# Gate and up blocks: one 512-column product per high weight tile, the halves of a result added on VectorE

## The chip, the cores and the metric

The kernel runs on one core of a Trainium2 chip, in one launch. The metric is the time of one execution in device microseconds (us), the median of three runs. Engines are named as in the profile: PE is TensorE (PEld its weight loads), DVE is VectorE, ACT is ScalarE, POOL is GpSimd, SP issues most of the DMAs. The memories are SBUF and, for products, PSUM (`ps`), in banks of 512 columns.

## The reference, cut to what matters

Two transformer blocks run one after the other on 256 tokens and 16 meta tokens, width 1024. The change touches the gated feed-forward at the end of the second block. There only the 256 real tokens count:

```python
f = rmsnorm_2(h, norm_ffn_g[i])
h = h + (jax.nn.silu(f @ w_gate[i]) * (f @ w_up[i])) @ w_down[i]
out = rmsnorm_2(h, norm_final_g)
```

`w_gate` and `w_up` are 1024 x 2816, `w_down` is 2816 x 1024, all float32. Everything ahead of it (a hybrid mixer, a retrieval of experts by gathers from memory, sparse attention, a convolution) is the same in both kernels.

## The kernel before, in words

Float32 products are made of three faster ones. Each operand is split into a high part, which is the value rounded to the type float32r, and a low part, the rest. The result is high x high + high weight x low operand + low weight x high operand.

Weights arrive from memory in blocks of 128 x 1024, which hold 128 output columns and all eight chunks `c` of the inner dimension. A ring has four slots for raw blocks (`ring`), and as many for the high parts (`w_hi`) and the low parts (`w_lo`). SP's queue loads a block when the low part of the block four before it has been made. ACT copies the high part (`split_hi`, L395). DVE subtracts to get the low part (`split_lo`, L403). Both helpers are called through `ahead(b)`, which treats block b + 2, two blocks ahead of the one in hand. A high copy may go once PE has begun the third block before it, since only then its slot is free.

The stage in question has 44 blocks, numbered from 0: in turns of four, two of gate and two of up. There are eleven turns. The first (turn 0) and, on DVE, the last (turn 10) are written out; the others are passes of a loop on the engine's sequencer. For each block PE runs 24 products of 256 columns (`column_block`, L624): for each c the high weights with the operand's high part (`peer_x[0]`, in `x_peer`) and with its low part (`peer_x[1]`, in `x_lo`), then for each c the low weights with the high part. They add up in one of four PSUM banks. Block 0 (`chunked_block`) has its products in another order, since it starts while its operand is still being made. Between turns 0 and 1 stand 16 small products of `open_sums` (L1080).

What happens to a finished tile k of a turn (k = 0 and 1 gate, 2 and 3 up) is ordered by the code of each engine, and each engine works in the order of its code. On DVE (`hidden_tiles`): `ahead` for the tile, which is the low part of block k + 2; then the product of tile and `rstd` out of PSUM (L2629), which frees the bank (`tile_taken`); then, for k = 2 and 3, gate times up (L2634), which gives a tile of `hidden`. On ACT (`gate_tiles`): `ahead` for the tile, then, for k = 0 and 1, Silu on what DVE has left (L1774). So ACT makes the high copy for tile k + 1 only behind the Silu of tile k, and DVE makes the low part, and takes the next tile, only behind that copy.

The 22 blocks of `w_down` follow (`row_tile`, L1093): per block 12 products of 512 columns, whose stationary operand is a piece of `hidden`, split by ACT (L1784) and DVE (L2610). The first two such subtractions stand in DVE's last turn of the stage, behind gate times up of tiles 2 and 3. ACT's first copies of this kind stand behind its last turn. After the last down block come a norm and the store.

Of the kernel before, what the change touches and what calls it, by code (L numbers as in the profile page):

```python
# [127 lines left out]
def build(nc, stream, rows_dram, small_dram, keys_dram, kiwi_dram, gain_dram, x_dram, gain_rows_dram, meta_2_dram, out_dram):  # L128
    with ExitStack() as ctx:
# [15 lines left out]
        x_hold = sb("x_hold", [P, C * T])  # L145
        x_lo = sb("x_lo", [P, C * T], F32R)
        x_peer = sb("x_peer", [P, C * REAL], F32R)
        peer_root = sb("peer_root", [P, 2])
# [106 lines left out]
        assert base <= one_at["sq"], base  # L255
        peer_x = (tokens_of(x_peer, REAL), tokens_of(x_lo, REAL))
        qp = route["qp"].rearrange("p (h t) -> p h t", h=PH)
        sc = route["sc"].rearrange("p (c n) -> p c n", c=CHAINS)
# [26 lines left out]
        QI, CU, CC, CB, KF, QF, GA, GB = 0, *range(4, 60, 8)  # L285
        ffa = carve([("ffa", FF * REAL), ("sg", 2 * REAL), ("up", 2 * REAL), ("out", 2 * D), ("gain", D), ("final_sq", 2 * D), ("final", 8)])
        hidden = ffa["ffa"].rearrange("p (n t) -> p n t", n=FF)
        sg = ffa["sg"].rearrange("p (n t) -> p n t", n=2)
        up = ffa["up"].rearrange("p (n t) -> p n t", n=2)
        out_tok = ffa["out"].rearrange("p (t n) -> p t n", t=2)  # L290
        final_sq = ffa["final_sq"].rearrange("p (t j n) -> p t j n", t=2, j=2)
# [16 lines left out]
        def rings_before(b):  # L308
# [22 lines left out]
            sem(n) for n in ("vbd_ready", "sb_out_ready", "sb_mixed", "pe_used_sp", "sp_hi_ready", "sp_lo_ready", "exact_ready"))  # L331
        z0_taken, q_zeroed = sem("z0_taken"), sem("q_zeroed")
        k_wide, wide_ready, wide_taken, mix_hi, mix_lo = (
# [34 lines left out]
        wi_turned, wi_taken = sem("wi_turned"), sem("wi_taken")  # L368
        vis_ready, padded = sem("vis_ready"), sem("padded")
        gate_silu, hidden_ready = sem("gate_silu"), sem("hidden_ready")  # L370
# [4 lines left out]


        X_MIX = 1
        X_CONV, X_ATTN = X_MIX + 1, X_MIX + 2
# [113 lines left out]
        def _(pool):  # L492
# [41 lines left out]

            g.memset(one["qall"], 0.0).then_inc(q_zeroed, 1)
            pool.wait_ge(q_zeroed, 1)
            g.memset(meta_both[PAIR:2 * PAIR, :], 0.0).then_inc(padded, 1)
            pool.wait_ge(padded, 1)
            g.memset(meta_both[2 * PAIR:P, :], 0.0).then_inc(padded, 1)
            pool.wait_ge(padded, 2)  # L540

# [32 lines left out]
            pool.wait_ge(vis_ready, 1)  # L574
            g.memset(pT[PAIR:2 * PAIR, :, 0:P], 0.0).then_inc(padded, 1)
            pool.wait_ge(padded, 3)
            g.memset(pT[2 * PAIR:P, :, 0:P], 0.0).then_inc(padded, 1)
            pool.wait_ge(padded, 4)

# [14 lines left out]
        def _(pe):  # L594
# [352 lines left out]

            def chunked_block(b0, g0, parts, at):

                parts_ready(b0)  # L950
                bank_is_free(pe, g0)
                out, k = bank_of(g0)[:, 0:REAL], b0 % RING
                for c in range(C - 1):
                    pe.wait_ge(peer_hi, at + c + 1)
                    i = mm(out, w_hi[:, k, c * P:(c + 1) * P], parts[0][:, c, :], start=c == 0, stop=False)
                    if c == 0:
                        i.then_inc(block_begun, 1)
                    mm(out, w_lo[:, k, c * P:(c + 1) * P], parts[0][:, c, :], start=False, stop=False)
                for c in range(C - 1):
                    pe.wait_ge(peer_lo, at + c + 1)  # L960
                    mm(out, w_hi[:, k, c * P:(c + 1) * P], parts[1][:, c, :], start=False, stop=False)
                c = C - 1
                pe.wait_ge(peer_hi, at + C)
                mm(out, w_hi[:, k, c * P:(c + 1) * P], parts[0][:, c, :], start=False, stop=False)
                mm(out, w_lo[:, k, c * P:(c + 1) * P], parts[0][:, c, :], start=False, stop=False)
                pe.wait_ge(peer_lo, at + C)
                mm(out, w_hi[:, k, c * P:(c + 1) * P], parts[1][:, c, :], start=False,
                   stop=True).then_inc(tile_ready, 1)

# [205 lines left out]
            pe.wait_ge(idx_taken, 16)  # L1175
            pe.wait_ge(padded, 4)
            attention_scores(0)
# [22 lines left out]
            b0, g0 = FIRST["w_gate_up_2"], TILE0["w_gate_up_2"]  # L1200
            chunked_block(b0, g0, peer_x, AT_FFN)
            norm(1, REAL)
            for n in range(1, RING):
                column_block(b0 + n, g0 + n, REAL, parts=peer_x)
            pe.wait_ge(root_ready, 2)
            open_sums(range(8))
            with pe.Fori(1, 2 * FF // RING) as i:
                for k in range(RING):
                    column_block(b0 + k, g0 + k, REAL, i, i, parts=peer_x)
            b0, turns = FIRST["w_down_2"], FF // RING  # L1210
# [12 lines left out]
        def _(act):  # L1223
# [596 lines left out]
        def _(dve):  # L1820
# [82 lines left out]
            def decayed_queries(begin, end):  # L1903

                if begin == 0:
                    dve.wait_ge(q_zeroed, 1)
                    for n in range(4):
                        tile_is_taken(dve, n)
# [838 lines left out]
```

## Time and profile before

| | |
|---|---|
| median of three runs | 1315.44 us (1315.14 to 1315.54) |
| span of the profiled execution, first to last instruction | 1313.5 us |
| median less that span | 1.94 us |
| mean granted TensorE clock | 0.992 of full speed |
| busy share of the span | PE 90%, DVE 68%, ACT 52%, POOL 21% |

No time of its own is known for the profiled execution beyond its span, so the 1.94 us between its span and the median stand for what lies around it. The span is what the rows below speak of; the clock is 1.00 in the whole stage of the change, from 1121.7 to 1248 us.

### The profile page before, as it was taken

What the parts mean: (1) busy time and instruction counts of PE and PEld (TensorE: products, weight loads), DVE (VectorE), ACT (ScalarE), POOL (GpSimd) and SP (SyncE); (2) the same over time, 40 slices, a digit from 0 to 9 for tenths busy, and PEclk for the clock granted to TensorE, in tenths of its full rate; (3) what the DMA queues carried; (4) which work ended last, traced back from release to release, by engine and by line L of the source; (5) the groups of instructions that cost most, each with busy time, mean ns of one, the idle gap of its engine ahead of it and who ended that gap; (6) DMA issues with size and microseconds to landing.
All of it is one profiled execution on the core that took longest, in us unless ns stands there. A gap on an engine that the chain in (4) does not pass through costs nothing.

```text
span 1313.5 us, 19083 instructions
## 1 busy us (share of the span) xinstructions
PE 1185.0 (90%) x6314; PEld 833.0 (63%) x6314; DVE 889.6 (68%) x1954; ACT 683.5 (52%) x1483; POOL 271.6 (21%) x307
## 2 busy tenths in 40 slices
PE   8999998987877788787888878999999999999998
PEld 6998964432322233333334322899999999999986
DVE  6764598866666667776677655577877667666664
ACT  6665565644444445554445544534456675434454
POOL 4000033443333333343434332000000020000000
PEclk9999999999999999999999999999999999999999
DMA  6422599999999999999999998546475355555562
GB/s 237 143 97 80 188 360 420 421 420 421 423 420 422 422 422 420 420 421 422 421 422 421 421 422 361 186 147 190 161 237 165 117 186 180 170 183 179 176 214 101
DMA packets 69060, 382.20 MB, mean 291 GB/s; under 512 B 7792, under 2 KB 7920, under 8 KB 36352
## 3 DMA queue, kind: packets, MB, share of 16 engines
q0 software_dynamic: 37152, 268.45, 49.2%
q1 hardware_dynamic: 30560, 108.90, 25.5%
q10 hardware_dynamic: 1280, 3.97, 0.9%
q8 instruction: 39, 0.64, 0.2%
q14 instruction: 29, 0.24, 0.1%
HBM read 380.24 MB, written 1.05 MB: 290 GB/s over the span
## 4 chain that ended last, share of the span: by engine, by line
PE 60%; DMA 25%; ACT 7%; DVE 5%; issue 3%; ACTq 0%; SPq 0%; DVEq 0%
PE ps L624 31%; DMA work<-in_rows,work 24%; PE ps L997 14%; PE ps L1093 5%; ACT work L1522 2%; DVE work L2246 2%; DMA ring<-in_stream 1%; ACT w_hi L395 1%; PE ps L657 1%; DVE w_lo L403 1%; PE ps L667 1%; PE ps L658 1%; ACT work L1518 1%; ACT work L1514 1%; PE ps L878 1%
## 5 line engine op out<-in xcount | busy, mean ns | idle before, releaser
L997 PE MATMUL ps<-work 128*128 128x512 f32 x1024 | 498.8, 621 | 112.1 <-ACT work L1522 111.8
L997 PEld LDWEIGHTS ps<-work 128*128 128x128 f32 x1024 | 182.1, 192 | 413.8 <-ACT work L1522 262.3
L2246 DVE CUSTOM_DVE_ANT_0 work<-work,ps 128x1024 f32<-128x1024 f32 x256 | 312.3, 1220 | 188.6 <-DMA work<-in_rows,work 187.8
L549 POOL DMA_INDIRECT work<-in_rows,work x254 | 243.4, 958 | 543.6 <-PE ps L997 379.4
L403 DVE TENSOR_TENSOR w_lo<-ring,w_hi 128x1024 fp32r<-128x1024 f32 x200 | 244.1, 1226 | 114.0 <-ACT w_hi L395 112.3
L624 PE MATMUL ps<-x_lo,w_hi 128*128 128x256 f32 (+2 forms) x1208 | 290.9, 283 | 1.0 <-DVE x_lo L420 0.9
L395 ACT ACTIVATE w_hi<-ring 128x1024 fp32r<-128x1024 f32 x200 | 208.5, 1053 | 55.4 <-PE ps L1093 24.5
L624 PEld LDWEIGHTS ps<-x_lo,w_hi 128*128 128x128 f32 x1208 | 226.4, 190 | 2.8 <-DVE x_lo L420 1.7
L1514 ACT ACTIVATE work<-work,peer_root 128x1 f32<-128x1 f32 x256 | 75.2, 294 | 279.2 <-DVE work L2246 278.6
L624 PE MATMUL ps<-x_hi,w_hi 128*128 128x256 f32 (+2 forms) x744 | 183.6, 289 | 1.5 <-ACT x_hi L413 0.9
L624 PEld LDWEIGHTS ps<-x_hi,w_hi 128*128 128x128 f32 x744 | 138.2, 189 | 6.0 <-issue 3.0
L1522 ACT ACTIVATE work<-ident,work 128x128 f32<-128x128 f32 x256 | 103.0, 403 | 24.9 <-PE ps L997 1.5
L624 PE MATMUL ps<-x_peer,w_hi 128*128 128x256 f32 x464 | 113.9, 287 | 0.0
L1251 ACT ACTIVATE work<-ps 128x256 f32<-128x256 f32 (+6 forms) x92 | 35.3, 384 | 136.2 <-PE ps L624 119.0
L624 PE MATMUL ps<-x_hi,w_lo 128*128 128x256 f32 (+2 forms) x744 | 104.3, 282 | 0.0
L624 PEld LDWEIGHTS ps<-x_hi,w_lo 128*128 128x128 f32 x744 | 95.6, 189 | 0.0
L624 PEld LDWEIGHTS ps<-x_peer,w_hi 128*128 128x128 f32 x464 | 88.0, 192 | 1.0 <-issue 0.7
L1518 ACT ACTIVATE work<-work 128x1 f32<-128x1 f32 x256 | 75.5, 295 | 9.3
L624 PE MATMUL ps<-x_peer,w_lo 128*128 128x256 f32 x464 | 65.1, 283 | 0.0
L624 PEld LDWEIGHTS ps<-x_peer,w_lo 128*128 128x128 f32 x464 | 59.9, 192 | 0.0
L583 POOL TENSOR_TENSOR work<-work 128x256 f32<-128x256 f32 x8 | 8.7, 1108 | 241.0 <-ACT work L1738 236.9
L1093 PE MATMUL ps<-w_hi,x_hi 128*128 128x512 f32 x176 | 47.5, 389 | 0.0
(398 smaller groups left out, 1225.4 us busy)
## 6 DMA issues: line engine op xcount, KB each, us to landing
ring<-in_stream SPq DMA_DIRECT2D x200, 512.0 KB, 3.6
work<-in_rows,work POOLq DMA_INDIRECT x254, 15.0
work<-in_stream ACTq DMA_DIRECT2D x4, 512.0 KB, 5.7
res<-in_tokens SPq DMA_DIRECT2D x4, 272.0 KB, 4.0
gain_rows<-in_gain_rows SPq DMA_DIRECT2D x1, 1024.0 KB, 9.6
x_hold<-in_stream ACTq DMA_DIRECT2D x2, 512.0 KB, 4.2
out_dram<-work SPq DMA_DIRECT2D x4, 256.0 KB, 2.3
keys_sb<-in_keys SPq DMA_DIRECT2D x1, 512.0 KB, 9.0
```

Source lines behind the costliest of these rows:

```text
L395: nc.scalar.activation(as_parked(b, w_hi[:, k, :]), raw_block(b), ACT.Copy).then_inc(w_hi_ready, 1)
L403: nc.vector.tensor_tensor(as_parked(b, w_lo[:, k, :]), raw_block(b), as_parked(b, w_hi[:, k, :].bitcast(F32)), ALU.subtract).then_inc(w_lo ...
L549: g.indirect_dma_start(out=gathered[:, n % ROWS, :], out_offset=None, in_=rows_dram, in_offset=bass.IndirectOffsetOnAxis(ap=expert[:, n:n ...
L624: last = mm(out, w[:, k, c * P:(c + 1) * P], x[:, c, skip:], start=n == 0, stop=n == 3 * C - 1)
L657: i = mm(out, xh[:, c, at:at + P], hi, start=c == 0, stop=False)
L997: last = mm(ps[:, Y_BANK[t] + j, :], diag[:, n % DIAGS, :], gathered[:, n % ROWS, D + 512 * j:D + 512 * j + 512], start=False, stop=k == S ...
L1093: last = mm(ps[:, 4 + 2 * t + j, :], x, w[:, k, 512 * j:512 * j + 512], start=False, stop=True, skip_group_check=True)
L1251: a(out, bank_of(g)[0:rows, 0:tokens], ACT.Copy).then_inc(tile_taken[BANK[g]], 1)
L1514: a(gelu, route["dot"][:, s:s + 1], ACT.Gelu, scale=peer_root[:, t:t + 1]).then_inc(gelu_ready, 1)
L1518: a(coef, gelu, ACT.Copy, scale=route["share"][:, s:s + 1]).then_inc(coef_ready, 1)
L1522: a(diag[:, s % DIAGS, :], ident[:, :], ACT.Copy, scale=coef).then_inc(diag_ready, 1)
L2246: v.tensor_tensor_reduce(u, u, ps[:, bank:bank + 2, :].rearrange("p b n -> p (b n)"), 1.0, 0.0, ALU.mult, ALU.add, R["dot"][:, s:s + 1]).t ...
```

## The change

The operand's high and low parts now lie side by side in one tensor, `x_wide`. A block's eight high weight tiles each meet both parts in one product of 512 columns: the left half of the bank (`HI_HALF`) takes high x high, the right half (`LO_HALF`) high weight x low operand. The low weights meet the high part as before, 256 columns wide, and add to the left half. So a block has 16 products where it had 24, of the same 6144 columns in all, and its result lies in two halves that have still to be added.

ACT copies the right half into SBUF (`low`). DVE adds the left half to that copy, which frees the bank, and then multiplies the sum by `rstd` in a second instruction (`summed`). Silu and gate times up wait for this second one. Block 0 keeps its 24 products, with the low operand's ones sent to the right half. Elsewhere only semaphores are merged (`q_zeroed` and `padded` into `zeroed`), which changes no instruction's order.

```diff
@@ -143,8 +143,8 @@
-        x_lo = sb("x_lo", [P, C * T], F32R)
-        x_peer = sb("x_peer", [P, C * REAL], F32R)
+        x_wide = sb("x_wide", [P, C * (REAL + T)], F32R)
+        x_peer, x_lo = x_wide[:, 0:C * REAL], x_wide[:, C * REAL:]
...
+        x_pairs = x_wide[:, 0:2 * C * REAL].rearrange("p (r n) -> p r n", r=2)
+        HI_HALF, LO_HALF = slice(0 * REAL, 0 * REAL + REAL), slice(1 * REAL, 1 * REAL + REAL)
...
+            def wide_block(b, g, turn=0, tile_turn=None):
+
+                pe.wait_ge(w_hi_ready, turn * RING + (b + 1))
+                bank_is_free(pe, g, tile_turn)
+                k, out = b % RING, bank_of(g)
+                for c in range(C):
+                    last = mm(out, w_hi[:, k, c * P:(c + 1) * P], x_pairs[:, :, REAL * c:REAL * c + REAL], start=c == 0,
+                              stop=c == C - 1)
+                    if c == 0:
+                        last.then_inc(block_begun, 1)
+                parts_ready(b, turn)
+                for c in range(C):
+                    last = mm(out[:, HI_HALF], w_lo[:, k, c * P:(c + 1) * P], peer_x[0][:, c, :], start=False,
+                              stop=True, skip_group_check=True)
+                last.then_inc(tile_ready, 1)
...
             for n in range(1, RING):
-                column_block(b0 + n, g0 + n, REAL, parts=peer_x)
+                wide_block(b0 + n, g0 + n)
...
                 for k in range(RING):
-                    column_block(b0 + k, g0 + k, REAL, i, i, parts=peer_x)
+                    wide_block(b0 + k, g0 + k, i, i)
...
+                    g = g0 + k
+                    act.wait_ge(tile_ready, t * RING + (g + 1))
+                    if turn is not None:
+                        act.wait_ge(summed, t * RING + (k + 1 - RING))
+                    a(low[:, k, :], bank_of(g)[:, LO_HALF], ACT.Copy).then_inc(low_ready, 1)
                     if k < 2:
-                        g = g0 + k
-                        act.wait_ge(tile_taken[BANK[g]], t + (ORD[g] + 1))
+                        act.wait_ge(summed, t * RING + (k + 1))
                         a(sg[:, k, :], sg[:, k, :], ACT.Silu).then_inc(gate_silu, 1)
...
-                    dve.wait_ge(tile_ready, i * RING + (g + 1))
-                    tt(sg[:, k, :] if k < 2 else up[:, k - 2, :], bank_of(g)[:, 0:REAL], rstd[:, 0:REAL],
-                       ALU.mult).then_inc(tile_taken[BANK[g]], 1)
+                    tile = sg[:, k, :] if k < 2 else up[:, k - 2, :]
+                    dve.wait_ge(low_ready, i * RING + (k + 1))
+                    tt(tile, bank_of(g)[:, HI_HALF], low[:, k, :], ALU.add).then_inc(tile_taken[BANK[g]], 1)
+                    dve.wait_ge(tile_taken[BANK[g]], i + (ORD[g] + 1))
+                    tt(tile, tile, rstd[:, 0:REAL], ALU.mult).then_inc(summed, 1)
                     if k > 1:
-                        dve.wait_ge(tile_taken[BANK[g]], i + (ORD[g] + 1))
+                        dve.wait_ge(summed, i * RING + (k + 1))
                         dve.wait_ge(gate_silu, i * 2 + (k - 1))
                         tt(hidden[:, i * 2 + (k - 2), :], up[:, k - 2, :], sg[:, k - 2, :],
                            ALU.mult).then_inc(hidden_ready, 1)
```

How the instructions stand on the engines now is shown at three places, each in the loop over turns 1 to 9 or 10. REGISTER_ALU and ISA are steps of the sequencer that work out what a semaphore is compared with.

On DVE, the steps for tiles 1 and 2 of a turn, from behind the low part of tile 1's step; before (L2629 the product with `rstd`, L403 the low part, L2634 gate times up):

```order
L2628 REGISTER_ALU [waits hidden_ready]
L2629 TENSOR_TENSOR work<-ps,spare 128x256 [waits tile_ready]
L402 REGISTER_ALU
L403 TENSOR_TENSOR w_lo<-ring,w_hi 128x1024 [waits w_hi_ready]
L2629 TENSOR_TENSOR work<-ps,spare 128x256 [waits tile_ready]
L2632 REGISTER_ALU
L2633 REGISTER_ALU [waits tile_taken2]
L2634 ISA [waits gate_silu]
L2634 TENSOR_TENSOR work<-work 128x256
```

and now, for the same two tiles (L2656 the sum of the halves, L2658 the product with `rstd`, L408 the low part, L2662 gate times up):

```order
L2655 REGISTER_ALU [waits hidden_ready]
L2656 TENSOR_TENSOR work<-ps,work 128x256 [waits low_ready]
L2658 TENSOR_TENSOR work<-work,spare 128x256 [waits tile_taken1]
L407 REGISTER_ALU
L408 TENSOR_TENSOR w_lo<-ring,w_hi 128x1024 [waits w_hi_ready]
L2655 REGISTER_ALU
L2656 TENSOR_TENSOR work<-ps,work 128x256 [waits low_ready]
L2657 REGISTER_ALU
L2658 TENSOR_TENSOR work<-work,spare 128x256 [waits tile_taken2]
L2661 REGISTER_ALU [waits summed]
L2662 ISA [waits gate_silu]
L2662 TENSOR_TENSOR work<-work 128x256
```

Each tile has one more DVE instruction, which waits for the sum just made (`tile_taken`), and gate times up waits for that one (`summed`) in place of the first.

On ACT, the high copies and Silus of tiles 0 and 1 of a turn; before (L395 a high copy, L1774 Silu):

```order
L395 ACTIVATE w_hi<-ring 128x1024 [waits block_begun]
L1773 REGISTER_ALU
L1774 ACTIVATE work<-work 128x256 [waits tile_taken0]
L394 REGISTER_ALU [waits landed3]
L395 ACTIVATE w_hi<-ring 128x1024 [waits block_begun]
L1774 ACTIVATE work<-work 128x256 [waits tile_taken1]
```

and now, the same two steps (L400 a high copy, L1797 the copy of a tile's right half, L1800 Silu):

```order
L400 ACTIVATE w_hi<-ring 128x1024 [waits block_begun]
L1794 REGISTER_ALU
L1796 REGISTER_ALU [waits tile_ready]
L1797 ACTIVATE work<-ps 128x256 [waits summed]
L1799 REGISTER_ALU
L1800 ACTIVATE work<-work 128x256 [waits summed]
L400 ACTIVATE w_hi<-ring 128x1024 [waits block_begun,landed3]
L1794 REGISTER_ALU
L1796 REGISTER_ALU [waits tile_ready]
L1797 ACTIVATE work<-ps 128x256 [waits summed]
L1799 REGISTER_ALU
L1800 ACTIVATE work<-work 128x256 [waits summed]
```

A copy out of PSUM stands ahead of each Silu, and Silu waits for `summed`, DVE's second instruction, where it waited for `tile_taken`, its first. The next high copy still stands behind Silu.

On PE, block 1 of a turn; before (of the eight pairs with high weights three rows are shown, then the eight with low weights):

```order
L609 REGISTER_ALU
L624 MATMUL ps<-x_peer,w_hi 128x256 [waits tile_taken1,w_hi_ready]
L624 MATMUL ps<-x_lo,w_hi 128x256
L624 MATMUL ps<-x_peer,w_hi 128x256
...
L624 MATMUL ps<-x_peer,w_lo 128x256 [waits w_lo_ready]
L624 MATMUL ps<-x_peer,w_lo 128x256 x7
```

and now, the whole block:

```order
L955 REGISTER_ALU
L959 MATMUL ps<-x_wide,w_hi 128x512 [waits tile_taken1,w_hi_ready]
L959 MATMUL ps<-x_wide,w_hi 128x512 x7
L965 MATMUL ps<-x_wide,w_lo 128x256 [waits w_lo_ready]
L965 MATMUL ps<-x_wide,w_lo 128x256 x7
```

The sixteen products with high weights have become eight of twice the width; the waits are the same.

## Rows read from the trace of the kernel before

**Rows 1.** The page: the span.

```profile
span 1313.5 us, 19083 instructions
```

**Rows 2.** The chain that ended last: start, duration, what ran.

```profile
...
1133.05 115.19 PE ps L624 x960
1248.25 59.88 PE ps L1093 x264
```

**Rows 3.** Waits from 1122 to 1250 us: total, times, longest.

```profile
ACT work L1774 <- DVE work L2629: 68.5, 21, 5.2
DVE work L2629 <- PE ps L624: 11.2, 20, 1.5
```

**Rows 4.** Timeline of PE: first product of a block, and of the fourth after.

```profile
1161.68 0.28 PE L624 MATMUL ps<-x_peer,w_hi 128*128 128x256 f32 x1
...
1173.20 0.28 PE L624 MATMUL ps<-x_peer,w_hi 128*128 128x256 f32 x1
```

**Rows 5.** Timeline of PE in the down blocks, 244 products between the two starts.

```profile
1248.09 0.63 PE L1093 MATMUL ps<-w_hi,x_hi 128*128 128x512 f32 x2
...
1303.42 1.07 PE L1093 MATMUL ps<-w_hi,x_hi 128*128 128x512 f32 x4
```

**Rows 6.** Timeline of DVE and ACT, one turn of four tiles, by start.

```profile
1159.01 0.42 DVE L2629 TENSOR_TENSOR work<-ps,spare 128x256 f32<-128x256 f32 x1 [0.59 <-PE ps L624]
1159.46 0.42 ACT L1774 ACTIVATE work<-work 128x256 f32<-128x256 f32 x1 [5.04 <-DVE work L2629]
1159.79 1.04 ACT L395 ACTIVATE w_hi<-ring 128x1024 fp32r<-128x1024 f32 x1
1160.86 1.22 DVE L403 TENSOR_TENSOR w_lo<-ring,w_hi 128x1024 fp32r<-128x1024 f32 x1 [1.43 <-ACT w_hi L395]
1162.00 0.42 DVE L2629 TENSOR_TENSOR work<-ps,spare 128x256 f32<-128x256 f32 x1
...
1165.00 0.42 DVE L2629 TENSOR_TENSOR work<-ps,spare 128x256 f32<-128x256 f32 x1
1165.65 0.42 DVE L2634 TENSOR_TENSOR work<-work 128x256 f32 x1 [0.23 <-DVE work L2629]
1165.99 1.22 DVE L403 TENSOR_TENSOR w_lo<-ring,w_hi 128x1024 fp32r<-128x1024 f32 x1
1167.65 0.42 DVE L2629 TENSOR_TENSOR work<-ps,spare 128x256 f32<-128x256 f32 x1 [0.44 <-PE ps L624]
1168.30 0.43 DVE L2634 TENSOR_TENSOR work<-work 128x256 f32 x1 [0.23 <-DVE work L2629]
1168.70 1.23 DVE L403 TENSOR_TENSOR w_lo<-ring,w_hi 128x1024 fp32r<-128x1024 f32 x1
1170.53 0.42 DVE L2629 TENSOR_TENSOR work<-ps,spare 128x256 f32<-128x256 f32 x1 [0.60 <-PE ps L624]
```

**Rows 7.** Timeline of DVE in the last turn, which stands outside the loop.

```profile
1245.71 0.42 DVE L2629 TENSOR_TENSOR work<-ps,spare 128x256 f32<-128x256 f32 x1
1246.16 0.42 DVE L2634 TENSOR_TENSOR work<-work 128x256 f32<-128x256 f32 x1
```

**Rows 8.** Timeline of ACT and DVE at the stage's start.

```profile
1123.66 1.28 ACT L1774 ACT_TABLE_LOAD   x1
1123.68 0.42 DVE L2629 TENSOR_TENSOR work<-ps,spare 128x256 f32<-128x256 f32 x1 [0.49 <-ACT spare L1246]
```

**Rows 9.** Groups by line, 1000 to 1313 us: copies out of PSUM on ACT.

```profile
L1251 ACT ACTIVATE work<-ps 128x256 f32<-128x256 f32 x19 | 7.3, 382 | 15.7 <-PE ps L624 15.7
```

**Rows 10.** Timeline and windows around two long PE pauses; PEclk is the third last number.

```profile
542.03 10.49 PE L997 MATMUL ps<-work 128*128 128x512 f32 x20 [5.25 <-ACT work L1522]
541.00:546.00 5.00, 3.97 (x6) 1.79 (x7) 4.38 (x13) 3.50 (x12) 0.07 (x1) 0.66 1.02 423
...
260.81 12.26 PE L997 MATMUL ps<-work 128*128 128x512 f32 x24 [3.10 <-ACT work L1522]
261.00:267.00 6.00, 6.00 (x11) 2.48 (x11) 3.90 (x10) 2.66 (x8) 1.46 (x2) 0.72 1.00 416
```

More of the change, by code:

```diff
@@ L285, in build @@
         QI, CU, CC, CB, KF, QF, GA, GB = 0, *range(4, 60, 8)
-        ffa = carve([("ffa", FF * REAL), ("sg", 2 * REAL), ("up", 2 * REAL), ("out", 2 * D), ("gain", D), ("final_sq", 2 * D), ("final", 8)])
+        ffa = carve([("ffa", FF * REAL), ("sg", 2 * REAL), ("up", 2 * REAL), ("low", RING * REAL), ("out", 2 * D), ("gain", D), ("final_sq", 2 * D), ("final", 8)])
         hidden = ffa["ffa"].rearrange("p (n t) -> p n t", n=FF)
@@ L289, in build @@
         up = ffa["up"].rearrange("p (n t) -> p n t", n=2)
+        low = ffa["low"].rearrange("p (n t) -> p n t", n=RING)
         out_tok = ffa["out"].rearrange("p (t n) -> p t n", t=2)
@@ L331, in build @@
             sem(n) for n in ("vbd_ready", "sb_out_ready", "sb_mixed", "pe_used_sp", "sp_hi_ready", "sp_lo_ready", "exact_ready"))
-        z0_taken, q_zeroed = sem("z0_taken"), sem("q_zeroed")
+        z0_taken = sem("z0_taken")
         k_wide, wide_ready, wide_taken, mix_hi, mix_lo = (
@@ L368, in build @@
         wi_turned, wi_taken = sem("wi_turned"), sem("wi_taken")
-        vis_ready, padded = sem("vis_ready"), sem("padded")
+        vis_ready = sem("vis_ready")
+        low_ready, summed = sem("low_ready"), sem("summed")
         gate_silu, hidden_ready = sem("gate_silu"), sem("hidden_ready")
@@ L373, in build @@
             sem(n) for n in ("gain_landed", "down_ready", "final_step", "final_rooted", "out_ready"))
+        Q_ZEROED = 15
         X_MIX = 1
@@ L533, in _ @@
                                 channel_multiplier=1).then_inc(consts, 1)
[L535 to L540, printed above, removed]
+            g.memset(one["qall"], 0.0).then_inc(zeroed, 1)
+            pool.wait_ge(zeroed, Q_ZEROED)
+            g.memset(meta_both[PAIR:2 * PAIR, :], 0.0).then_inc(zeroed, 1)
+            pool.wait_ge(zeroed, Q_ZEROED + 1)
+            g.memset(meta_both[2 * PAIR:P, :], 0.0).then_inc(zeroed, 1)
+            pool.wait_ge(zeroed, Q_ZEROED + 2)
             for n in range(SLOTS - 2):
@@ L574, in _ @@
             pool.wait_ge(vis_ready, 1)
[L575 to L578, printed above, removed]
+            g.memset(pT[PAIR:2 * PAIR, :, 0:P], 0.0).then_inc(zeroed, 1)
+            pool.wait_ge(zeroed, Q_ZEROED + 3)
+            g.memset(pT[2 * PAIR:P, :, 0:P], 0.0).then_inc(zeroed, 1)
+            pool.wait_ge(zeroed, Q_ZEROED + 4)
             for n in range(C):
@@ L946, in _ @@
             b0, g0 = FIRST["w_peer_q"], TILE0["w_peer_q"]
-            def chunked_block(b0, g0, parts, at):
+            def wide_block(b, g, turn=0, tile_turn=None):
[12 more added lines that the diff above has]
+                last.then_inc(tile_ready, 1)
@@ L950, in chunked_block @@
+            def chunked_block(b0, g0, parts, at, halves=None):
                 parts_ready(b0)
                 bank_is_free(pe, g0)
-                out, k = bank_of(g0)[:, 0:REAL], b0 % RING
+                k, split = b0 % RING, halves is not None
+                out, out_lo = (bank_of(g0)[:, half] for half in halves or (slice(0, REAL), slice(0, REAL)))
                 for c in range(C - 1):
                     pe.wait_ge(peer_hi, at + c + 1)
-                    i = mm(out, w_hi[:, k, c * P:(c + 1) * P], parts[0][:, c, :], start=c == 0, stop=False)
+                    i = mm(out, w_hi[:, k, c * P:(c + 1) * P], parts[0][:, c, :], start=c == 0, stop=False, skip_group_check=split)
@@ L956, in chunked_block @@
                     if c == 0:
                         i.then_inc(block_begun, 1)
-                    mm(out, w_lo[:, k, c * P:(c + 1) * P], parts[0][:, c, :], start=False, stop=False)
+                    mm(out, w_lo[:, k, c * P:(c + 1) * P], parts[0][:, c, :], start=False, stop=False, skip_group_check=split)
                 for c in range(C - 1):
                     pe.wait_ge(peer_lo, at + c + 1)
-                    mm(out, w_hi[:, k, c * P:(c + 1) * P], parts[1][:, c, :], start=False, stop=False)
+                    mm(out_lo, w_hi[:, k, c * P:(c + 1) * P], parts[1][:, c, :], start=False, stop=False, skip_group_check=split)
@@ L962, in chunked_block @@
                 c = C - 1
                 pe.wait_ge(peer_hi, at + C)
-                mm(out, w_hi[:, k, c * P:(c + 1) * P], parts[0][:, c, :], start=False, stop=False)
-                mm(out, w_lo[:, k, c * P:(c + 1) * P], parts[0][:, c, :], start=False, stop=False)
+                mm(out, w_hi[:, k, c * P:(c + 1) * P], parts[0][:, c, :], start=False, stop=False, skip_group_check=split)
+                mm(out, w_lo[:, k, c * P:(c + 1) * P], parts[0][:, c, :], start=False, stop=False, skip_group_check=split)
@@ L966, in chunked_block @@
                 pe.wait_ge(peer_lo, at + C)
-                mm(out, w_hi[:, k, c * P:(c + 1) * P], parts[1][:, c, :], start=False,
-                   stop=True).then_inc(tile_ready, 1)
+                mm(out_lo, w_hi[:, k, c * P:(c + 1) * P], parts[1][:, c, :], start=False,
+                   stop=True, skip_group_check=split).then_inc(tile_ready, 1)
             def sum_squares():
@@ L1175, in _ @@
             pe.wait_ge(idx_taken, 16)
-            pe.wait_ge(padded, 4)
+            pe.wait_ge(zeroed, Q_ZEROED + 4)
             attention_scores(0)
@@ L1200, in _ @@
             b0, g0 = FIRST["w_gate_up_2"], TILE0["w_gate_up_2"]
-            chunked_block(b0, g0, peer_x, AT_FFN)
+            chunked_block(b0, g0, peer_x, AT_FFN, halves=(HI_HALF, LO_HALF))
             norm(1, REAL)
             for n in range(1, RING):
-                column_block(b0 + n, g0 + n, REAL, parts=peer_x)
+                wide_block(b0 + n, g0 + n)
             pe.wait_ge(root_ready, 2)
@@ L1905, in decayed_queries @@
                 if begin == 0:
-                    dve.wait_ge(q_zeroed, 1)
+                    dve.wait_ge(zeroed, Q_ZEROED)
                     for n in range(4):
```

## The prediction

> **What bounds the kernel now.** I read the chain that ended last first, since it tells which stretch the change can shorten. From 1133 us on it is PE alone: 115.19 us of gate and up products in one piece, then 59.88 us of down products [rows 2]. The span ends at 1313.5 us [rows 1]. So in this stage PE is never kept waiting, and a faster PE would shorten the span as long as the others keep up.
>
> Whether they do is read from the waits and from one turn on DVE and ACT. DVE waited 11.2 us for PE in the stage, in 20 places, and ACT 68.5 us for DVE [rows 3]. The reader is to see in the turn [rows 6] that DVE waits for PE only at two tiles of four, 0.44 and 0.60 us, and is otherwise driven by a chain that passes to and fro between DVE and ACT. PE paces the turn by a small margin, and that margin is the question.
>
> PE's pace: four blocks take 1173.20 - 1161.68 = 11.52 us, for 96 products, so 0.120 us for one of 256 columns [rows 4]. In the down blocks 244 products of 512 columns take 1303.42 - 1248.09 = 55.33 us, 0.2268 us each [rows 5].
>
> **PE's part of the change.** A wide block is 8 x 0.2268 + 8 x 0.120 = 2.774 us, where 24 x 0.120 = 2.880 was: 0.106 us less, or 4.6 us over 43 blocks. A turn on PE falls from 11.52 to 11.10 us. The moving operand now comes in two pieces of 256 columns; no row has that, and I price it from both sides: nothing (0.2268 us) or as much as two products (0.240). By the higher one a turn is again 11.52.
>
> **The chain's part.** Start to start in rows 6, for tiles 0 and 1: product to Silu 0.45 (1159.01, 1159.46), Silu to high copy 0.33 (1159.79), high copy to low part 1.07 (1160.86), low part to the next tile's product 1.14 (1162.00). That is 2.99 us a tile. For tiles 2 and 3 ACT has no Silu and runs ahead, and the chain is DVE's own work: product to gate times up 0.65, that to the low part 0.34 (tile 2) or 0.40 (tile 3, where the loop turns), then 1.14: 2.13 and 2.19. The turn sums to 2 x 2.99 + 2.13 + 2.19 = 10.30 us. PE's 11.52 hides it with 1.22 to spare.
>
> The change puts a second DVE instruction into each of the four steps, and both the Silu and gate times up wait for this one. Its length is 0.42 us by the products of the same shape, but what counts is how soon a DVE instruction can follow one whose result it waits for. The rows have two prices. In the written-out last turn it is 0.45 (1245.71, 1246.16) [rows 7]; in the loop it is 0.65, with 0.23 of idle time [rows 6]. The order shows the difference: in the loop gate times up has two sequencer steps, one of which itself waits for the product, ahead of it, while the new multiply waits by itself and has at most a step ahead that waits for nothing. Such a step also stands between gate times up and the low part, which follow one another in 0.34 [rows 6], so it hides. I take 0.45 and keep 0.65 for the range. Gate times up keeps its form and its 0.65.
>
> The turn of the chain is then 10.30 + 4 x 0.45 = 12.10 us: 3.44, 3.44, 2.58 and 2.64. That is more than PE's 11.10, and more than the 11.52 of before. **So the chain becomes the bound, and PE's gain goes into waiting for weights**: block b + 2 can't begin before the step of tile b has made its parts. It also makes the 0.2268 or 0.240 of the wide products indifferent.
>
> ACT's copies of the right halves cost 0.38 us each [rows 9], 1.5 a turn. They lie beside DVE's 1.14 us of making a low part, since each stands right behind the high copy that this low part waited for. Without that cover they would add 0.38 to two or more steps. The loads of raw blocks wait for low parts made four blocks before, 12 us, and stay hidden.
>
> **The sum along the chain.** Before, the first product started at 1123.68 and the table for Silu was loaded from 1123.66 for 1.28 us [rows 8]. Now ACT first copies the right half of tile 0, 0.38, so the first sum starts at about 1124.07 and Silu at 1123.66 + 0.38 + 1.28, about 1125.35. With 0.33 + 1.07 + 1.14 tile 1's sum is at 1127.89, tile 2's 3.44 later at 1131.33; in this written-out turn the next two steps are 0.45 + 0.45 + 0.34 + 1.14 = 2.38, so turn 1 begins at 1136.09. Nine turns of 12.10 bring turn 10 to 1244.99, and its tiles 1 and 2 to 1248.43 and 1251.87. The sum, its multiply and gate times up of tile 2 (2 x 0.45), then 0.34 to the subtraction that gives the first down block its operand, and 0.5 until PE sees it: 1253.6. Before, the down products began at 1248.09 [rows 5]. They are 5.5 us later, and from there to the end of the span PE is as busy as it was: span 1319.0.
>
> **The hand-over.** PE's last gate and up block needs the parts made in tile 1's step of turn 10, its high part at 1244.99 + 0.45 + 0.45 + 0.33 + 1.07 = 1247.29; it ends 2.77 later at 1250.06. So PE stands idle for 3.5 us ahead of the down blocks. Pauses of 3.10 and 5.25 us in this trace were both followed by a stretch at the lower of the clock's two levels, 1.2 GHz for 2.4: the granted clock is 0.72 over the 6 us and 0.66 over the 5 us around them [rows 10], which is 6 x 0.28 = 1.68 and 5 x 0.34 = 1.70 us of full clock lost. The down blocks are PE's alone, so the loss would reach the end. I count it as the likelier: 1319.0 + 1.7 = 1320.7 of span, and with the 1.94 us that lie between the span and the median (1315.44), **1322.6 us**.
>
> **The rivals.** *The clock holds.* The pause has to reach the length after which the two above fell; 3.5 is near the shorter one. Then 1320.9.
>
> *The new multiply costs 0.65 in the loop too*, if the sequencer's step before it delays it. Nine turns of 4 x 0.20 are 7.2 us more: 1329.8 with the lower clock, 1328.1 without.
>
> *Waiting for one's own result costs nothing.* If a DVE instruction could follow its source as soon as an independent one does, 0.34 [rows 6], each multiply would add 0.34, and gate times up would come 0.31 sooner: 10.30 + 4 x 0.34 - 2 x 0.31 = 11.04 us. That is just under PE's 11.10, and PE would be the bound again. It decides from there, at a chain of 11.10. PE gains 4.6 us but pays at the hand-over: the copy of the first down operand on ACT now stands behind the copy of tile 43's right half, so three short instructions (0.38, about 0.4 and 0.42) lie between PE's last block and the first down product, 1.3 to 2.1 us with their signals. The time is then 1315.44 - 4.6 + 1.3 to 2.1, 1312.1 to 1312.9: not slower. The Trainium skill, "VectorE: DVE Perf Modes", section "The DRAIN you can't avoid", has such a rule: copies with a semaphore after each took as long as copies with one at the end, so "the semaphore costs nothing extra here". By that rule this rival would hold. The trace is against it, with 0.45 and 0.65 between dependent instructions where independent ones are 0.34 apart [rows 6, 7].
>
> *Nothing comes of it*: the chain falls behind more slowly than I sum, by signals that I count twice, and ends near 11.5 a turn; 1314 to 1317.
>
> **How the numbers follow.** Chain-bound with the lower clock 0.55, chain-bound at full clock 0.20, the multiply at 0.65 0.11, waiting for nothing 0.06, near no change 0.08. The prediction is that of the first. The range runs from 1319.5, which leaves out the last two, to 1330.0, which holds the dearer multiply: 0.86 less what a miss in the sums takes. A measurement of this kernel can tell about 0.2% (2.6 us) from no change. Slower by more: the first three, 0.86; within: the fifth and half of the fourth, 0.10; faster by more: 0.04.
>
> **What would show it.** Right: the DVE chain without a wait for PE from the middle of the stage on, 12.1 us from a sum to that of the fourth tile after; add to multiply 0.45; PE with a pause at a wide block's first or second half, near 1.0 us a turn, and one of about 3.5 us ahead of the down blocks; a wide product at 0.227 us where PE isn't waiting. Wrong: a turn of 11.1 with DVE still waiting for PE (waiting costs nothing), of 12.9 (0.65), or wide products above 0.26 us, which would make PE the bound after all. The clock's part is seen in the granted clock of the first down blocks.

## The result and the profile after

The change made the kernel slower: the median is 1322.81 us (6 runs, 1319.15 to 1324.21) against 1315.29 us of the kernel before in the same session (6 runs, 1313.94 to 1316.10). The ratio is 1.0054, with a 95% interval of 1.0043 to 1.0065. The prediction was 1322.6 us, with a range of 1319.5 to 1330.0. The profiled execution took 1322.71 us; its page gives a span 7.3 us longer than that of [rows 1]:

```profile
span 1320.8 us, 18600 instructions
```

**Who bounds the stage.** The chain that ended last (start, duration, what ran), where [rows 2] showed one piece of PE work up to the down products:

```profile
1229.50 1.22 DVE w_lo L408
1241.64 1.22 DVE w_lo L408
...
1253.99 61.48 PE ps L1115 x264
```

From 1133 us on it was PE without a break; now it passes through DVE's low parts, one every 12.14 us (1229.50, 1241.64). PE comes back into it only at the down products, which start at 1253.99 where they started at 1248.09 [rows 5]: 5.90 us later.

The waits from 1122 to 1256 us (in total, times, longest), answering to [rows 3]:

```profile
ACT work L1800 <- DVE work L2658: 51.0, 21, 3.6
DVE w_lo L408 <- ACT w_hi L400: 31.8, 22, 1.7
...
PE ps L1115 <- DVE x_hi L2636: 3.2, 1, 3.2
PE ps L959 <- ACT w_hi L400: 2.8, 6, 0.5
```

DVE's 20 waits for PE are gone. In their place PE waits: for high parts of weights in the loop, and once for 3.2 us ahead of the down blocks.

**One turn on DVE and ACT**, from the timeline, answering to [rows 6]. L2656 is the sum of the two halves, L2658 the new multiply, L2662 gate times up, L408 a low part; on ACT, L1800 is Silu, L400 a high copy, L1797 the copy of a right half:

```profile
1160.45 0.42 DVE L2656 TENSOR_TENSOR work<-ps,work 128x256 f32<-128x256 f32 x1
1160.90 0.42 DVE L2658 TENSOR_TENSOR work<-work,spare 128x256 f32<-128x256 f32 x1
1161.36 0.42 ACT L1800 ACTIVATE work<-work 128x256 f32<-128x256 f32 x1 [2.92 <-DVE work L2658]
1162.64 0.36 ACT L1797 ACTIVATE work<-ps 128x256 f32<-128x256 f32 x1
1162.77 1.23 DVE L408 TENSOR_TENSOR w_lo<-ring,w_hi 128x1024 fp32r<-128x1024 f32 x1 [1.44 <-ACT w_hi L400]
1163.91 0.42 DVE L2656 TENSOR_TENSOR work<-ps,work 128x256 f32<-128x256 f32 x1
...
1167.36 0.42 DVE L2656 TENSOR_TENSOR work<-ps,work 128x256 f32<-128x256 f32 x1
1167.81 0.42 DVE L2658 TENSOR_TENSOR work<-work,spare 128x256 f32<-128x256 f32 x1
1168.46 0.42 DVE L2662 TENSOR_TENSOR work<-work 128x256 f32 x1 [0.23 <-DVE work L2658]
1169.94 0.42 DVE L2656 TENSOR_TENSOR work<-ps,work 128x256 f32<-128x256 f32 x1
...
1172.59 0.42 DVE L2656 TENSOR_TENSOR work<-ps,work 128x256 f32<-128x256 f32 x1
```

From sum to sum the four steps are 3.46 (1160.45 to 1163.91), 3.45, 2.58 (1167.36 to 1169.94) and 2.65, together 12.14 us (1160.45 to 1172.59), where 10.30 of chain stood behind 11.52 of PE. Sum to multiply is 0.45 and multiply to Silu 0.46 (1160.90, 1161.36). The copy of the right half starts at 1162.64 and ends at 1163.00, while DVE makes the low part from 1162.77 to 1164.00: it adds nothing to the step.

**PE**, from the timeline: a stretch early in the stage, where it isn't waiting yet, and one turn apart in the middle, answering to [rows 4]:

```profile
1152.19 2.00 PE L959 MATMUL ps<-x_wide,w_hi 128*128 128x512 f32 x8
1154.04 1.12 PE L965 MATMUL ps<-x_wide,w_lo 128*128 128x256 f32 x8
1154.99 2.00 PE L959 MATMUL ps<-x_wide,w_hi 128*128 128x512 f32 x8
...
1163.37 2.00 PE L959 MATMUL ps<-x_wide,w_hi 128*128 128x512 f32 x8
...
1178.45 2.09 PE L959 MATMUL ps<-x_wide,w_hi 128*128 128x512 f32 x8 [0.47 <-ACT w_hi L400]
...
1190.59 0.72 PE L959 MATMUL ps<-x_wide,w_hi 128*128 128x512 f32 x2 [0.47 <-ACT w_hi L400]
```

A block takes 2.80 us (1152.19 to 1154.99): eight wide products in 1.85 and eight narrow ones in 0.95, 0.231 and 0.119 us each. Four such blocks are 11.18 us (1152.19 to 1163.37), but from 1178.45 to 1190.59 a turn takes 12.14: PE stands still for 0.96 us of it, of which the profile names 0.47 as a wait for a high part.

### The profile page after: what moved, and what is told of

It is laid out like the page before. It is cut to its first block, busy times and chain, and to the rows that moved or that the text cites. A ratio compares the mean times of both kernels' runs of the same rounds, so it can differ in the third digit from the quotient of the medians.

```text
span 1320.8 us, 18600 instructions
## 1 busy us (share of the span) xinstructions
PE 1186.8 (90%) x5970; PEld 817.9 (62%) x5970; DVE 906.1 (69%) x1998; ACT 695.5 (53%) x1527; POOL 271.1 (21%) x307
## 4 chain that ended last, share of the span: by engine, by line
PE 49%; DMA 25%; DVE 10%; ACT 9%; issue 6%; DVEq 0%; ACTq 0%; SPq 0%
DMA work<-in_rows,work 24%; PE ps L629 22%; PE ps L1019 13%; PE ps L1115 5%; ACT w_hi L400 3%; DVE w_lo L408 2%; DVE work L2272 2%; ACT work L1544 2%; DVE work L2658 1%; DVE work L2656 1%; DMA ring<-in_stream 1%; PE ps L662 1%; ACT work L1540 1%; ACT work L1536 1%; PE ps L672 1%
## 5 line engine op out<-in xcount | busy, mean ns | idle before, releaser
L408 DVE TENSOR_TENSOR w_lo<-ring,w_hi 128x1024 fp32r<-128x1024 f32 x200 | 244.0, 1225 | 113.3 <-ACT w_hi L400 111.6
L400 ACT ACTIVATE w_hi<-ring 128x1024 fp32r<-128x1024 f32 x200 | 209.6, 1052 | 55.0 <-PE ps L1115 24.8
L629 PE MATMUL ps<-x_wide,w_hi 128*128 128x256 f32 (+2 forms) x984 | 211.6, 284 | 1.0 <-DVE x_wide L425 0.9
L629 PEld LDWEIGHTS ps<-x_wide,w_hi 128*128 128x128 f32 x984 | 168.4, 190 | 3.7 <-DVE x_wide L425 1.7
L959 PE MATMUL ps<-x_wide,w_hi 128*128 128x512 f32 x344 | 87.8, 397 | 2.8 <-ACT w_hi L400 2.8
L959 PEld LDWEIGHTS ps<-x_wide,w_hi 128*128 128x128 f32 x344 | 61.7, 188 | 16.5 <-issue 4.2
L965 PEld LDWEIGHTS ps<-x_wide,w_lo 128*128 128x128 f32 x344 | 46.9, 190 | 3.4
L965 PE MATMUL ps<-x_wide,w_lo 128*128 128x256 f32 x344 | 47.9, 282 | 0.0
```

Source lines behind the costliest of these rows:

```text
L400: nc.scalar.activation(as_parked(b, w_hi[:, k, :]), raw_block(b), ACT.Copy).then_inc(w_hi_ready, 1)
L408: nc.vector.tensor_tensor(as_parked(b, w_lo[:, k, :]), raw_block(b), as_parked(b, w_hi[:, k, :].bitcast(F32)), ALU.subtract).then_inc(w_lo ...
L629: last = mm(out, w[:, k, c * P:(c + 1) * P], x[:, c, skip:], start=n == 0, stop=n == 3 * C - 1)
L959: last = mm(out, w_hi[:, k, c * P:(c + 1) * P], x_pairs[:, :, REAL * c:REAL * c + REAL], start=c == 0, stop=c == C - 1)
L965: last = mm(out[:, HI_HALF], w_lo[:, k, c * P:(c + 1) * P], peer_x[0][:, c, :], start=False, stop=True, skip_group_check=True)
```

## The experiments

One measure serves most of them. The work ahead of the stage ends up to 2 us earlier or later from one profiled execution to another (the first wide block starts between 1120.44 and 1122.59 us in the traces here), so I compare **the stage alone: from the start of the first wide block to that of the first down product**. In the changed kernel it is 1253.99 - 1122.34 = 131.65 us. In the kernel before, the same block (block 1) starts here, by the timeline of PE:

```profile
1122.33 0.47 PE L624 MATMUL ps<-x_peer,w_hi 128*128 128x256 f32 x1
```

So its stage is 1248.09 [rows 5] - 1122.33 = 125.76 us. A table behind the experiments has the measure for all kernels.

### The new multiply left out

```diff
...
-                        act.wait_ge(summed, t * RING + (k + 1))
+                        act.wait_ge(tile_taken[BANK[g]], t + (ORD[g] + 1))
...
-                    dve.wait_ge(tile_taken[BANK[g]], i + (ORD[g] + 1))
-                    tt(tile, tile, rstd[:, 0:REAL], ALU.mult).then_inc(summed, 1)
...
```

> Leaves out the multiply of gate and up by rstd: the sum of the halves goes straight to Silu and to gate times up. Theory (the chain between DVE and ACT is the bound, and the second DVE instruction put it above PE's pace): the chain's turn is 10.3 us again, PE sets the pace with 11.2 us a turn, and only the hand-over to the down blocks is late, by 1.5 to 2 us: about 1313.5 us. Rival (the wide products or the copies out of PSUM slow the stage): stays at 1320 or more.

Measured: 1312.97 us (1311.96 to 1313.64), ratio 0.9984 to before (0.9975 to 0.9993). The timeline of PE, first down product:

```profile
1245.01 0.73 PE L1115 MATMUL ps<-w_hi,x_hi 128*128 128x512 f32 x2 [1.24 <-DVE x_hi L2636]
```

The stage takes 123.44 us, 8.2 less than in the changed kernel, and the blocks run at PE's own 2.79 us each. The loss hangs on this one instruction per tile, though DVE was busy for only 69% of the changed kernel's span. What is left at the hand-over, from the gate and up blocks to the down blocks, is a wait of 1.24 us.

### The wide products alone

```diff
...
-                    a(low[:, k, :], bank_of(g)[:, LO_HALF], ACT.Copy).then_inc(low_ready, 1)
...
-                    tt(tile, bank_of(g)[:, HI_HALF], low[:, k, :], ALU.add).then_inc(tile_taken[BANK[g]], 1)
-                    dve.wait_ge(tile_taken[BANK[g]], i + (ORD[g] + 1))
-                    tt(tile, tile, rstd[:, 0:REAL], ALU.mult).then_inc(summed, 1)
+                    dve.wait_ge(tile_ready, i * RING + (g + 1))
+                    tt(tile, bank_of(g)[:, HI_HALF], rstd[:, 0:REAL], ALU.mult).then_inc(tile_taken[BANK[g]], 1)
...
```

> Wide products alone: the right halves are neither copied nor added (so high weight x low operand is left out of the result), DVE multiplies the left half by rstd as in the kernel before. Theory: PE paces every turn at about 11.2 us and the hand-over is as before, about 1312.0 us, 3.4 us under the kernel before. Rival (a moving operand in two pieces costs as much as two products): 1315.4, no gain.

Measured: 1311.21 us (1310.86 to 1313.90), ratio 0.9973 (0.9961 to 0.9985).

The stage is 122.04 us, and PE does not wait ahead of the down products. So PE's part of the change is a gain of 3.8 us over the kernel before of the same session (1315.02 - 1311.21); by the stage it is 3.72 (125.76 - 122.04). What the two halves need on ACT and DVE takes it back, and 7.5 us more.

### The moving operand in one piece

Against the kernel just above:

```diff
-                    last = mm(out, w_hi[:, k, c * P:(c + 1) * P], x_pairs[:, :, REAL * c:REAL * c + REAL], start=c == 0,
+                    last = mm(out, w_hi[:, k, c * P:(c + 1) * P], x_wide[:, 2 * REAL * c:2 * REAL * (c + 1)], start=c == 0,
```

> As the wide products alone, but the moving operand of each wide product is one piece of 512 neighbouring columns (so it meets the wrong parts of the operand; the right halves are left out too). Theory (the two pieces cost the 4 ns by which a wide product of the changed kernel, 0.231 us, is above the 0.2268 of the down blocks): 0.227 us each and about 1310.5 us, 1.5 under the wide products alone. Rival (the pieces cost nothing, the 4 ns come from elsewhere): 1312.0.

Measured: 1311.76 us (1310.35 to 1312.40), ratio 0.9975 (0.9963 to 0.9986). The timeline of PE, one block:

```profile
1162.06 2.00 PE L959 MATMUL ps<-x_wide,w_hi 128*128 128x512 f32 x8
1163.90 0.28 PE L965 MATMUL ps<-x_wide,w_lo 128*128 128x256 f32 x1
```

Here the rival holds. The stage takes 122.03 us, against 122.04 with two pieces, and the eight wide products still take 1.84 us (1162.06 to 1163.90), 0.230 each. Two pieces of 256 columns cost PE nothing. The 3 to 4 ns by which a wide product exceeds the 0.2268 us of the down blocks have another cause, which no run here shows.

### A third dependent instruction

```diff
...
                     tt(tile, tile, rstd[:, 0:REAL], ALU.mult).then_inc(summed, 1)
+                    dve.wait_ge(summed, i * (2 * RING) + (2 * k + 1))
+                    tt(tile, tile, rstd[:, 0:REAL], ALU.mult).then_inc(summed, 1)
...
```

The waits for `summed` are counted anew to match.

> The changed kernel with a third DVE instruction per tile, one more multiply by rstd that waits for the second (so gate and up are scaled twice). Theory (what counts is the chain, 0.45 us for each instruction that waits for the one before): the turn grows from 12.14 to 13.94 us, and the time by about 19 us, to 1342. Rival (DVE has room, since it is busy for some 9 us of 12; its waits for ACT take the extra work up): within 3 us of 1322.8.

Measured: 1342.07 us (1341.81 to 1342.60), ratio 1.0205 (1.0189 to 1.0221). The timeline of DVE:

```profile
1163.76 0.42 DVE L2656 TENSOR_TENSOR work<-ps,work 128x256 f32<-128x256 f32 x1
1164.21 0.42 DVE L2658 TENSOR_TENSOR work<-work,spare 128x256 f32<-128x256 f32 x1
1164.67 0.43 DVE L2660 TENSOR_TENSOR work<-work,spare 128x256 f32<-128x256 f32 x1
...
1177.74 0.42 DVE L2656 TENSOR_TENSOR work<-ps,work 128x256 f32<-128x256 f32 x1
```

The three follow one another by 0.45 and 0.46, and a turn takes 13.98 us (1163.76 to 1177.74): 1.84 more than 12.14, 0.46 a tile. Each further dependent instruction is paid in full at every tile, which it could not be if the chain did not set the pace.

### The high copy ahead of Silu

ACT makes the next block's high copy before it waits for the tile's multiply; nothing is left out.

```diff
+                if turn is not None:
+                    ahead(b0, t)
                 for k in range(RING):
-                    if k or turn is not None:
-                        ahead(b0 + k, t)
...
                     a(low[:, k, :], bank_of(g)[:, LO_HALF], ACT.Copy).then_inc(low_ready, 1)
+                    if k < RING - 1:
+                        ahead(b0 + k + 1, t)
                     if k < 2:
                         act.wait_ge(summed, t * RING + (k + 1))
                         a(sg[:, k, :], sg[:, k, :], ACT.Silu).then_inc(gate_silu, 1)
```

> The changed kernel with one difference: on ACT the next high copy stands ahead of Silu. Nothing is left out. Theory (it is the order, the high copy behind a Silu that waits for DVE's second instruction): DVE's own turn is about 9.2 us, PE sets the pace at 11.2 us, the hand-over stays 1.5 to 2 us late: about 1313.7 us. Rival (DVE simply has too much work with four more instructions a turn): 1320 to 1323, as the changed kernel.

Measured: 1313.43 us (1312.21 to 1314.97), ratio 0.9987 (0.9978 to 0.9996). The waits from 1122 to 1250 us, and then the timeline of DVE (L2658 and L2660 are here the sum and the multiply):

```profile
ACT work L1797 <- PE ps L965: 51.1, 41, 3.3
DVE work L2658 <- ACT work L1797: 16.5, 24, 2.1
```

```profile
1161.53 0.42 DVE L2658 TENSOR_TENSOR work<-ps,work 128x256 f32<-128x256 f32 x1 [0.62 <-ACT work L1797]
1161.98 0.43 DVE L2660 TENSOR_TENSOR work<-work,spare 128x256 f32<-128x256 f32 x1
...
1172.70 0.42 DVE L2658 TENSOR_TENSOR work<-ps,work 128x256 f32<-128x256 f32 x1 [0.62 <-ACT work L1797]
```

The same instructions are there, with the same 0.45 between sum and multiply, yet DVE now waits 0.6 us for a copy of a right half, which itself waits for PE; a turn is 11.17 us, PE's own. So the length of DVE's instructions alone was not what made the change slow: the chain that passed from the multiply through Silu and the high copy to the low part was. The stage is again 123.44 us, with the same 1.24 us at the hand-over as without the multiply.

The same order in the kernel before, where PE set the pace:

```diff
+                if turn is not None:
+                    ahead(b0, t)
                 for k in range(RING):
-                    if k or turn is not None:
-                        ahead(b0 + k, t)
+                    if k < RING - 1:
+                        ahead(b0 + k + 1, t)
```

> The kernel before with the high copy ahead of Silu, nothing else. Theory (before, PE sets the pace and the chain has 1.2 us to spare): 1315.4, no difference. Rival (the order is worth something by itself): 1313 or less.

Measured: 1315.19 us (1314.12 to 1316.94), ratio 1.0001 (0.9992 to 1.0010). The waits from 1122 to 1250 us, answering to [rows 3]:

```profile
ACT work L1776 <- DVE work L2631: 36.8, 20, 2.2
ACT w_hi L395 <- PE ps L624: 31.3, 20, 3.6
```

ACT waits half as long for DVE (36.8 us, where it was 68.5), and the time now appears as waits for PE. The stage is 125.76 us in both orders. Taking a chain apart that PE hides gives nothing.

### PE kept at work over the hand-over

Fourteen products that nobody reads stand ahead of the down blocks.

```diff
+            pe.wait_ge(tile_taken[BANK[g0]], FF // 2 + ORD[g0])
+            for n in range(14):
+                mm(bank_of(g0), w_hi[:, RING - 1, n % C * P:(n % C + 1) * P], x_pairs[:, :, REAL * (n % C):REAL * (n % C) + REAL],
+                   start=True, stop=True)
```

> The changed kernel with 14 products of 512 columns more, whose results are not used, between the gate and up blocks and the down blocks, where PE stands idle for 3.2 us. Theory (the pause lowers the clock, which costs 1.3 to 1.7 us of the down blocks): granted clock 1.00 in the first down blocks and 1321.2 us, some 1.5 under the changed kernel. Rival (the clock there makes no difference to the end): 1322.8, or later if the fillers get in the way.

Measured: 1321.05 us (1320.29 to 1321.49), ratio 1.0043 (1.0030 to 1.0057). The interval overlaps that of the changed kernel, so the traces must tell. The timeline of PE, and below it a window of 1 us right after its down products began (PEclk is the third number from the right):

```profile
1249.28 3.36 PE L1234 MATMUL ps<-x_wide,w_hi 128*128 128x512 f32 x14
1252.67 0.50 PE L1115 MATMUL ps<-w_hi,x_hi 128*128 128x512 f32 x1
```

```profile
1253.00:1254.00 1.00, 1.00 (x6) 0.81 (x5) 1.00 (x2) 0.73 (x1) 0.00 (x0) 1.00 0.84 344
```

The stage takes 131.69 us, as long as without the filler (131.65). From the first down product to the end of the span it is 65.5 us (1318.2 - 1252.67) where the changed kernel takes 66.8 (1320.8 - 1253.99) and the kernel before took 65.4 (1313.5 - 1248.09). The lower clock, and not the pause itself, is what those 1.3 us were lost to.

### Both ends mended

The high copy ahead of Silu as above; besides, ACT makes the first down operands before its last turn, and DVE's side of them moves from the steps of the last turn's tiles 2 and 3 to those of tiles 0 and 1. Nothing is left out.

```diff
...
-            with act.Fori(1, FF // 2) as i:
+            with act.Fori(1, FF // 2 - 1) as i:
                 gate_tiles(i)
...
+            for k in range(RING):
+                act.wait_ge(hidden_ready, k + 1)
+                row_hi(hidden[:, k, :], FIRST["w_down_2"] + k)
+            gate_tiles(FF // 2 - 1)
...
-                        if rows:
-                            row_lo(hidden[:, k - 2, :], HIDDEN0 + k - 2, d0 + k - 2)
+                    elif rows:
+                        row_lo(hidden[:, k, :], HIDDEN0 + k, d0 + k)
```

> The high copy ahead of Silu, and the hand-over mended: ACT copies the first four tiles of hidden for the down blocks ahead of its last turn, and DVE subtracts the first two in the steps of tiles 0 and 1 of its last turn. Nothing is left out. Theory: PE's pace throughout, no pause at the hand-over, about 1312.0 us, faster than both kernels. Rival (the chain comes back elsewhere, as by Silu being later): 1313.7 or more.

Measured: 1311.68 us (1310.30 to 1312.47), ratio 0.9973 (0.9962 to 0.9985): faster than both kernels, by 3.4 us and by 11.1. The timeline of PE:

```profile
1242.17 1.12 PE L965 MATMUL ps<-x_wide,w_lo 128*128 128x256 f32 x8
1243.12 0.63 PE L1115 MATMUL ps<-w_hi,x_hi 128*128 128x512 f32 x2
```

The last block runs into the down products without a wait, and the stage is 122.03 us, that of the wide products alone. The whole gain that PE's part holds is there, with both halves still added.

### The stage in all kernels

Worked out from the timelines of PE and the spans, in us:

| kernel | first wide block (before: block 1) | first down product | stage | idle ahead of it | from there to the span's end |
|---|---|---|---|---|---|
| before | 1122.33 | 1248.09 | 125.76 | none | 65.4 |
| before, high copy first | 1122.10 | 1247.86 | 125.76 | none | 65.3 |
| changed | 1122.34 | 1253.99 | 131.65 | 3.24 | 66.8 |
| multiply left out | 1121.57 | 1245.01 | 123.44 | 1.24 | 65.5 |
| wide products alone | 1121.96 | 1244.00 | 122.04 | none | 65.3 |
| operand in one piece | 1121.04 | 1243.07 | 122.03 | none | 65.3 |
| third instruction | 1120.44 | 1271.53 | 151.09 | 4.15 | 68.3 |
| high copy first | 1122.59 | 1246.03 | 123.44 | 1.24 | 65.5 |
| filler | 1120.98 | 1252.67 | 131.69 | filled | 65.5 |
| both ends mended | 1121.09 | 1243.12 | 122.03 | none | 65.3 |

## Why the prediction was right

**The chain.** A turn was to take 12.10 us, in steps of 3.44, 3.44, 2.58 and 2.64, and it took 12.14, in 3.46, 3.45, 2.58 and 2.65. The choice that carried this was 0.45 us for the multiply, of the two prices in [rows 6, 7]. The third instruction measured it again, at 0.46. The 0.65 of gate times up is still there (1167.81 to 1168.46), behind its sequencer step that waits, while the multiply, which waits by itself, never took it: that rival is refuted. That the extra 0.20 of gate times up comes from that step fits every row here, but no run moved the wait to show it.

The rival by which waiting for one's own result costs nothing wanted a turn of about 11.1 and DVE still waiting for PE; it is refuted too. The Trainium skill, "VectorE: DVE Perf Modes", section "The DRAIN you can't avoid", found that eight copies with a semaphore after each took as long as eight with one at the end; no run here repeats that, and the section does not say that a copy there waited for the result of the one before it. An instruction that does so followed here by 0.45 us, where an independent one follows by 0.34 [rows 6].

**The start.** The first sum and the first Silu were to start at about 1124.07 and 1125.35, and turn 1 at 1136.09. The timeline of DVE, answering to [rows 8]:

```profile
1124.13 0.42 DVE L2656 TENSOR_TENSOR work<-ps,work 128x256 f32<-128x256 f32 x1 [0.94 <-ACT work L1797]
...
1136.13 0.42 DVE L2656 TENSOR_TENSOR work<-ps,work 128x256 f32<-128x256 f32 x1
```

The sum starts at 1124.13 and turn 1 at 1136.13; Silu, on ACT, starts at 1125.34.

**The hand-over.** Turn 10 was to begin at 1244.99 and the down products at 1253.6. The timelines of PE and of DVE (L2636 is the subtraction that gives the down block its operand), answering to [rows 5, 7]:

```profile
1247.69 2.11 PE L959 MATMUL ps<-x_wide,w_hi 128*128 128x512 f32 x8
1249.64 1.11 PE L965 MATMUL ps<-x_wide,w_lo 128*128 128x256 f32 x8
1253.99 0.80 PE L1115 MATMUL ps<-w_hi,x_hi 128*128 128x512 f32 x1 [3.24 <-DVE x_hi L2636]
```

```profile
1245.36 0.42 DVE L2656 TENSOR_TENSOR work<-ps,work 128x256 f32<-128x256 f32 x1
...
1253.52 0.42 DVE L2636 TENSOR_TENSOR x_hi<-work,x_hi 128x256 fp32r<-128x256 f32 x1
```

They came at 1245.36 and 1253.99: the 0.04 us by which each of nine turns was longer had added up. The shift of the down products is so 5.90 us and not 5.5. The stage began at the same time in both profiled executions (1122.33 and 1122.34), so the whole shift is the stage's own. PE's pause is 3.24 us and not 3.5: its last block began 0.40 later than predicted (1247.69 against 1247.29) and took 3.06 us to the end of its last product (1250.75), where 2.77 was the time from one block's start to the next's.

**The clock.** It fell, as I held likelier. The windows over the hand-over, answering to [rows 10], and below them one of the kernel before, just ahead of the work that resumed there at 542.03:

```profile
1253.00:1254.00 1.00, 0.01 (x1) 0.01 (x1) 0.96 (x4) 1.00 (x2) 0.00 (x0) 0.72 0.53 86
1254.00:1255.00 1.00, 1.00 (x2) 0.82 (x3) 1.00 (x2) 0.24 (x2) 0.00 (x0) 0.50 0.98 381
1255.00:1256.00 1.00, 1.00 (x4) 0.79 (x3) 0.93 (x4) 1.00 (x2) 0.00 (x0) 0.50 0.15 57
1256.00:1257.00 1.00, 1.00 (x4) 0.78 (x3) 1.00 (x3) 0.25 (x1) 0.00 (x0) 0.58 0.71 184
1257.00:1258.00 1.00, 1.00 (x6) 0.80 (x5) 1.00 (x2) 0.00 (x0) 0.00 (x0) 1.00 0.87 340
```

```profile
541.00:542.00 1.00, 0.00 (x0) 0.00 (x0) 0.76 (x5) 0.88 (x4) 0.00 (x0) 0.97 1.02 426
```

The granted clock is at half, the 1.2 GHz level, until the window from 1256 us. Full clock lost is 0.28 + 0.50 + 0.50 + 0.42 = 1.70 us (one less the granted clock, window by window), the figure predicted from [rows 10]. But the 0.28 lie in a window in which PE is busy for 0.01 us: the fall came while it still stood idle (in windows of 0.2 us, between 1253.4 and 1253.6), and cost nothing there. Left are 1.4 us, which agrees with the 1.3 that the filler gave back. **This is the term that was mis-sized**: the clock lost in a window was taken for time lost. In the stretches of [rows 10] the two were nearly the same, since almost all of the loss fell on a PE at work (0.03 us of it ahead of 542.03, none ahead of 260.81); here the clock fell while PE had no work.

**The sum.** 5.90 + 1.4 is the 7.3 us by which the span grew; the prediction had 5.5 + 1.7. Two errors of 0.4 and 0.3 us, one each way, leave the total at 1322.6 against 1322.81; that they cancel so nearly is luck.

**PE's part.** A wide product was priced at 0.2268 to 0.240 us and took 0.230 or 0.231, so a block took 2.80 us instead of 2.774. As predicted this was indifferent while the chain set the pace. It matters for the versions in which PE does so again: 43 blocks x (2.880 - 2.795) = 3.7 us of gain where the prediction had 4.6. The stage of the last kernel, with both ends mended, is shorter than that of the kernel before by as much (125.76 - 122.03), and its time by 3.4 us.

The rivals of no change (a turn near 11.5) and of a clock that holds fell with the same rows. One term of a rival is met elsewhere: three short instructions at the hand-over were to cost 1.3 to 2.1 us once PE sets the pace. In the two kernels in which it does and they stand there (the multiply left out; the high copy first) PE waited 1.24, and the stage is 1.40 us longer than with the wide products alone (123.44 - 122.04), at the low end of that range.

## What to carry to other kernels

Before giving the bounding engine less to do, add up the chain that the others run beside it, start to start through every wait, and see by how much it is hidden: here 1.22 us a turn, and 4 x 0.45 us of new dependent instructions ate it. Busy shares did not tell (DVE 69%); the order in which an in-order engine takes its waits did, since the high copy queued behind a Silu that waited, and moving it ahead won back 9.4 us with the same work. And where one stage feeds the next, look at the last tile by itself: a pause of 3.2 us there cost 1.4 more through the clock. Moving the high copy left 1.24 us of the pause and no such loss, and making the operands earlier removed the rest.

## What the runs showed of the hardware

- A moving operand of two pieces of 256 columns, read as one of 512, costs PE the same as one contiguous piece: 122.03 and 122.04 us for the stage.
- A product of 512 columns took 0.230 or 0.231 us in these blocks and 0.2268 in the down blocks [rows 5], contiguous or not. Why is open.
- After the idle stretch of 3.24 us the granted clock was 0.50, the 1.2 GHz level, while PE already worked without a break, and 1.00 from the window of 1257 us on. After those of 1.24 us no such loss is seen (65.5 us to the end of the span, as with the filler). After that of 4.15 us, behind the third instruction, the clock was still at 0.50 in the window from 1276 us, and the rest took 68.3 us.
